# Recurrence of a delta-rule mixer: the two chains' level products issued chain by chain instead of kind by kind

## The chip, the cores and the metric

The kernel runs on one core of a Trainium2 chip. The metric is the device time of one execution in microseconds (us), lower is better. PE is the matmul engine (TensorE), DVE is VectorE, ACT is ScalarE, POOL is GpSimd, SP issues the DMAs.

## The reference

A block of two layers at 1024 tokens and width 1024. Layer 0 mixes tokens with a gated linear recurrence (eight heads of 64, run forwards and backwards) beside a dilated attention; layer 1 mixes with a Fourier transform; a convolved gated feed-forward follows each. The change touches the recurrence alone:

```python
def step(state, inp):
    r_t, w_t, k_t, v_t, kk_t, a_t = inp
    sk = jnp.einsum('bhij,bhj->bhi', state, kk_t)
    state = (state * w_t[:, :, None, :]
             - sk[..., :, None] * (kk_t * a_t)[:, :, None, :]
             + v_t[..., :, None] * k_t[:, :, None, :])
    y = jnp.einsum('bhij,bhj->bhi', state, r_t)
    return state, y
...
for d in range(2):
    ...
    y = y + wkv7_scan(rh, hs(decay), kd, vh, kk, ah, reverse=(d == 1))
```

## The kernel before

The engines run programs of their own, in order, and wait for each other by semaphores. The order of work is written out by hand in nested loops of each engine's program. In the function `recurrence` the 1024 steps are cut into 16 chunks of 64, and two chunks make a **pair step**, m = 0 to 7 (`NPAIR` is 8). Within a pair step there are two **chains**, g = 0 (forwards) and g = 1 (backwards), which share no data.

In a chunk the delta rule needs the inverse of a unit triangular 64x64 matrix, for 8 units (heads times halves) and 2 chunks. It is built up from 2x2 blocks (`X1`, `U1`) in five **levels**, i = 0 to 4 (`LEVELS` = 2, 4, 8, 16, 32). One level of one chain is, in this order of dependence:

- X product on PE (`level_x`, L1553): the chunk's matrix times the inverse so far, which is read from `T` (from `X1` at level 0). It writes PSUM bank 3 of the chain.
- XL copy on DVE (`level_x`, L1807): a predicated copy of bank 3 into `XL`.
- T product (L1572) and then U product (L1581) on PE (`level_tu`): both need the XL copy and the U copy of the level below.
- T copy on DVE (`level_t`, L1813 at level 0, L1815 at levels 1 to 3), for the next level's X product.
- U copy on ACT (`level_u`, L1668 at level 0, L1670 above).

Level 4 has no T product and no T copy. Each of these products is 32 matmul records in the trace for one chain: 64x64 weights, moving operands 32 columns wide, and 64 wide for T and U at level 0.

Beside the levels the engines prepare the next pair step's inputs (**side work**), for each chain: DVE `f_scan` (L1839), `f_centre` (L1845, L1847), `f_shift` (L1852), `f_alphas` (L1860 to L1864) and `f_nbetas` (L1869), handed out by `beside(m, slot)` in ten slots, slot 0 ahead of the pair step; ACT `f_rates` (L1690, four for each chain) and `f_exps` (L1698 to L1702); POOL `f_products` (L1745, L1746), behind `f_rates`, and `f_outputs` (L1752, L1755), behind `f_exps`. In pair step 7 there is none.

After the levels each pair step has `solve` (L1590), `carry` (L1599) and, for each chunk and chain, `step` (L1612 to L1625); ahead of them `turn`, `scores`, `lower`, `values`.

Of the kernel before, what the change touches and what calls it, by code (L numbers as in the profile page):

```python
# [539 lines left out]
NPAIR = NCH // 2  # L540
# [802 lines left out]
def recurrence(nc, z_d, vr_d, lw_d, aa_d, kk_d, tab, consts, ff, ysum, low, mix_out, bon_d, gate_d, yb_d, factors):  # L1343
# [6 lines left out]
    NL = len(LEVELS)  # L1350
    UN = 2 * KU
    HC = CH // 2
    with ExitStack() as ctx:
# [50 lines left out]
        def side(c):  # L1404
            return slice((1 - c) * CH, (2 - c) * CH)
# [16 lines left out]
        def bank(g, k):  # L1422
            return pb[:, 4 * g + k, :]
# [64 lines left out]
        def _(pe):  # L1488
# [53 lines left out]
            def level_x(g, m, i):  # L1542
                b = LEVELS[i]
                src = X1[g] if i == 0 else T[g]
                if i == 0:
                    pe.wait_ge(x1_c[g], 2 * m + 2)
                else:
                    pe.wait_ge(t_c[g], 4 * m + i)
                for u in range(UN):
                    hh, f = divmod(u, KU)  # L1550
                    for c in range(2):
                        out = bank(g, 3)[side(c), u * HC:(u + 1) * HC].rearrange("p (q b) -> p q b", b=b)
                        ins = mm(out, xn[g][side(c), hh, 2 * f + c, 0:CH], cols1(src[side(c), u, :], b, 0), start=True, stop=True)  # L1553
                ins.then_inc(x_done[g], 1)
# [74 lines left out]
            for m in range(NPAIR):  # L1629
                for phase in (turn, scores, lower, values):  # L1630
                    for g in range(2):
                        phase(g, m)
                for i in range(NL):
                    for g in range(2):
                        level_x(g, m, i)
                    for g in range(2):
                        level_tu(g, m, i)
                for phase in (solve, carry):
                    for g in range(2):
                        phase(g, m)  # L1640
                for c in range(2):
                    for g in range(2):
                        step(g, m, c)

        @block.scalar
        def _(act):
            A = nc.scalar.activation

            def tokens(g, m):
                for c in range(2):  # L1650
                    act.wait_ge(turned[g], 4 * m + c + 1)
                    A(xn[g][:, :, c::2, 2 * CH:3 * CH], bank(g, c).rearrange("p (f h e) -> p h f e", f=KU, h=2), ACT.Copy).then_inc(tok_c[g], 1)
                act.wait_ge(turned[g], 4 * m + 3)
                A(units(rz[g][:, :, 0:CH]), bank(g, 2).rearrange("p (f h e) -> p h f e", f=KU, h=2), ACT.Copy).then_inc(tok_c[g], 1)
                act.wait_ge(turned[g], 4 * m + 4)
                for c in range(2):
                    src = bank(g, 3)[other(c), :].rearrange("p (f h e) -> p h f e", f=KU, h=2)
                    A(units(wv[g][other(c), c, :, :]), src, ACT.Copy).then_inc(tok_c[g], 1)

            def values(g, m):  # L1660
                act.wait_ge(mv_done[g], m + 1)
                A(rz[g][:, :, CH:2 * CH], bank(g, 2).rearrange("p (u e) -> p u e", u=UN), ACT.Copy).then_inc(mv_c[g], 1)

            def level_u(g, m, i):
                b = LEVELS[i]
                act.wait_ge(u_done[g], NL * m + i + 1)
                if i == 0:
                    A(U[g][:, :, :], bank(g, 1).rearrange("p (u e) -> p u e", u=UN), ACT.Copy).then_inc(u_c[g], 1)  # L1668
                else:
                    A(cols(U[g][:, :, :], b, 1), narrow(g, 1, b), ACT.Copy).then_inc(u_c[g], 1)  # L1670

            def solved(g, m):
                act.wait_ge(z_done[g], m + 1)
                both_banks = pb[:, 4 * g + 2:4 * g + 4, :].rearrange("p h (f n) -> p h f n", f=KU)
                A(units(zt[g][:, :, :]), both_banks[:, :, :, 0:CH], ACT.Copy).then_inc(z_c[g], 1)
                for c in range(2):
                    A(units(wv[g][side(c), c, :, :]), both_banks[side(c), :, :, CH:2 * CH], ACT.Copy).then_inc(z_c[g], 1)

            def out(g, m, c):
                n = 2 * m + c  # L1680
                act.wait_ge(step_done[g], n + 1)
                A(ysum[:, g, :, n * CH:(n + 1) * CH], bank(g, 2 * c + 1)[:, 0:KU * CH].rearrange("p (f t) -> p f t", f=KU), ACT.Copy).then_inc(y_c[g], 1)

            def f_rates(g, m):
                act.wait_ge(ka_set, 1)
                if m:
                    act.wait_ge(f_loaded[g], 80 * m)
                    act.wait_ge(f_kappa[g], m)
                for f in range(KU):
                    ins = A(kd[g][:, f, :], aa[g][:, f, :], ACT.Identity, scale=vec[:, K_A, f:f + 1], bias=rest_ka[:, f:f + 1])  # L1690
                ins.then_inc(f_rate[g], 1)

            def f_exps(g, m):
                act.wait_ge(f_centred[g], m + 1)
                if m:
                    act.wait_ge(f_rho[g], m)
                    act.wait_ge(f_ends[g], m)
                A(emid[g][:, :, :], mids[g][:, :, :], ACT.Exp, scale=DECAY)  # L1698
                A(e1[g][:, :, :], cc[g][:, :, :], ACT.Exp, scale=DECAY).then_inc(f_exp[g], 1)
                act.wait_ge(f_before[g], m + 1)  # L1700
                A(lw[g][:, :, :], lw[g][:, :, :], ACT.Exp, scale=DECAY).then_inc(f_exp[g], 1)
                A(cc[g][:, :, :], cc[g][:, :, :], ACT.Exp, scale=-DECAY).then_inc(f_exp[g], 1)  # L1702

            for g in range(2):
                f_rates(g, 0)
            for g in range(2):
                f_exps(g, 0)
            for m in range(NPAIR):
                for phase in (tokens, values):
                    for g in range(2):  # L1710
                        phase(g, m)
                for i in range(NL):
                    for g in range(2):
                        level_u(g, m, i)
                    if m + 1 < NPAIR:
                        if i == 0:
                            for g in range(2):
                                f_rates(g, m + 1)
                        elif i <= 2:
                            f_exps(i - 1, m + 1)  # L1720
                for g in range(2):
                    solved(g, m)
                for c in range(2):
                    for g in range(2):
                        out(g, m, c)
            for g in range(2):
                act.wait_ge(y_c[g], 2 * NPAIR)
# [37 lines left out]
        def _(dve):  # L1765
# [33 lines left out]
            def level_x(g, m, i):  # L1799
                b = LEVELS[i]  # L1800
                if m == 0 and i < 2:
                    dve.wait_ge(filled_p, 2)
                if m == 0 and i == 2:
                    dve.wait_ge(filled_v, 1)
                dve.wait_ge(x_done[g], NL * m + i + 1)
                mask = level[:, i, :].rearrange("p (u q b) -> p u q b", u=1, b=b).broadcast_to([P, UN, HC // b, b])
                V.copy_predicated(cols(XL[i][g][:, :, :], b, 0), mask, narrow(g, 3, b)).then_inc(x_c[g], 1)  # L1807
# [63 lines left out]
            def beside(m, slot):  # L1871

                order = ((f_scan, 0), (f_scan, 1), (f_centre, 0), (f_centre, 1), (f_shift, 0), (f_shift, 1), (f_alphas, 0), (f_alphas, 1),
                         (f_nbetas, 0), (f_nbetas, 1))
                if m + 1 < NPAIR:
                    step, g = order[slot]
                    step(g, m + 1)
# [12 lines left out]
            for m in range(NPAIR):  # L1890
                beside(m, 0)
                for phase in (scores, lower, upper):
                    for g in range(2):
                        phase(g, m)
                for i in range(NL):
                    for g in range(2):
                        level_x(g, m, i)
                    beside(m, 2 * i + 1)
                    if i < NL - 1:
                        for g in range(2):  # L1900
                            level_t(g, m, i)
                        beside(m, 2 * i + 2)
                for g in range(2):
                    carry(g, m)
                for c in range(2):
                    for g in range(2):
                        advance(g, m, c)
# [1687 lines left out]
```

## Time and profile before

| | us |
|---|---|
| median of the 3 timed runs | 2850.46 (2849.05 to 2860.39) |
| profiled execution, first to last instruction | 2846.2 |
| recurrence, from the first X product of pair step 0 to the end of pair step 7 | about 440 |
| PE busy, whole kernel | 2625.7 (92%) |

The profiled execution has no device time of its own on record; its span of 2846.2 us lies 4.3 us under the median, which is time outside the first and last instruction and the spread of runs. A busy PE in such a table only says that matmul records follow one another: they overlap in the pipeline, so what a block of matmuls costs is read from the starts of successive blocks.

### The profile page before, as it was taken

To read this page: it belongs to the slowest core of one execution; us is meant where nothing else is said; L and a number is where in the kernel's file an instruction comes from. 1 tells how busy PE (TensorE), PEld (TensorE's weight loads), DVE (VectorE), ACT (ScalarE), POOL (GpSimd) and SP (SyncE) were. 2 spreads that over 40 slices of the span, in tenths; PEclk is the share of its full clock that TensorE was granted. 3 is DMA by queue.
4 is the path that set the end of the run, shared out by engine and by line. 5 is a ranking of instruction groups with operands and counts; after the bars stand their busy time and mean duration, and the time that the engine had idled before them with its cause. 6 is when DMAs were issued, how large, how long until landed. Compare 5 with 4: busy or idle time off the path is not lost. (4 is left out here: it accounts for less than half of the span.)

```text
span 2846.2 us, 54939 instructions
## 1 busy us (share of the span) xinstructions
PE 2625.7 (92%) x23187; PEld 2149.5 (76%) x23187; DVE 1603.8 (56%) x2296; ACT 1138.0 (40%) x1802; POOL 918.1 (32%) x625
## 2 busy tenths in 40 slices
PE   5998998896999999979999999997897999999998
PEld 5776556576989888758888888875776888888887
DVE  7775532457555544666555564455655555556445
ACT  4211342553344333344444444454434444444434
POOL 2302121104112210225877770000412777773000
PEclk9999999898999999989999999997998999999999
DMA  6676434602311220422222228543122222225654
GB/s 232 229 270 215 168 133 175 186 17 64 92 48 48 71 91 27 133 80 69 89 83 77 86 90 284 169 164 109 52 92 71 89 89 74 82 89 216 191 181 145
DMA packets 295928, 346.48 MB, mean 122 GB/s; under 512 B 28384, under 2 KB 224213, under 8 KB 295685
## 3 DMA queue, kind: packets, MB, share of 16 engines
q1 hardware_dynamic: 286044, 336.64, 36.6%
q10 hardware_dynamic: 9640, 6.33, 0.7%
q8 instruction: 185, 3.03, 0.4%
q14 instruction: 59, 0.48, 0.1%
HBM read 271.58 MB, written 71.34 MB: 120 GB/s over the span
## 5 line engine op out<-in xcount | busy, mean ns | idle before, releaser
L2847 POOL TENSOR_TENSOR cg_u_lo<-cg_u_raw,cg_u_hi 128x512 fp32r<-128x512 f32 x210 | 315.2, 1509 | 146.8 <-ACT cg_u_hi L2733 146.8
L131 PE MATMUL cg_ps<-m_hi,cg_u_hi 128*128 128x512 f32 x844 | 331.2, 392 | 26.0 <-DVE cg_u_lo L2922 21.7
L133 PE MATMUL cg_ps<-m_hi,cg_u_lo 128*128 128x512 f32 x844 | 330.0, 391 | 0.0
L132 PE MATMUL cg_ps<-m_lo,cg_u_hi 128*128 128x512 f32 x808 | 315.5, 390 | 0.0
L2733 ACT ACTIVATE cg_u_hi<-cg_u_raw 128x512 fp32r<-128x512 f32 x216 | 132.1, 629 | 380.5 <-PE cg_ps L133 229.8
L131 PEld LDWEIGHTS cg_ps<-m_hi,cg_u_hi 128*128 128x128 f32 x844 | 159.7, 189 | 61.1 <-DVE cg_u_lo L2922 22.5
L131 PE MATMUL cg_ps<-over_y_tx,cg_u_hi 128*128 128x512 f32 x480 | 186.7, 389 | 0.0
L132 PE MATMUL cg_ps<-over_y_tx,cg_u_hi 128*128 128x512 f32 x480 | 186.7, 389 | 0.0
L133 PE MATMUL cg_ps<-over_y_tx,cg_u_lo 128*128 128x512 f32 x480 | 186.7, 389 | 0.0
L133 PEld LDWEIGHTS cg_ps<-m_hi,cg_u_lo 128*128 128x128 f32 x844 | 159.5, 189 | 33.5
L2899 DVE SCALAR_TENSOR_TENSOR cg_z<-cg_ps,top_conv_f,cg_z 128x1023 f32<-128x1023 f32 x88 | 113.0, 1284 | 115.1 <-ACT cg_z L2757 115.1
L132 PEld LDWEIGHTS cg_ps<-m_lo,cg_u_hi 128*128 128x128 f32 x808 | 152.7, 189 | 31.8
L2847 POOL TENSOR_TENSOR cg_u_lo<-cg_u_s,cg_u_hi 128x512 fp32r<-128x512 f32 x80 | 103.7, 1296 | 63.5 <-ACT cg_u_hi L2733 63.5
L1745 POOL TENSOR_TENSOR rw_kd<-rw_kd,att_kx 128x512 f32<-128x512 f32 x16 | 24.7, 1543 | 280.1 <-ACT rw_kd L1690 280.1
L2902 DVE SCALAR_TENSOR_TENSOR cg_z<-cg_ps,top_conv_f,cg_z 128x1023 f32<-128x1023 f32 x88 | 112.9, 1283 | 3.1
L131 PE MATMUL za_ps<-h_hi,za_w_hi 128*128 128x512 f32 x256 | 103.7, 405 | 8.2 <-POOL za_w_lo L1029 8.2
L2757 ACT ACTIVATE cg_z<-cg_ps,top_conv_f 128x1024 f32<-128x1024 f32 x88 | 98.1, 1115 | 21.0 <-DVE cg_ps L2959 11.6
L132 PEld LDWEIGHTS cg_ps<-over_y_tx,cg_u_hi 128*128 128x128 f32 x480 | 90.1, 188 | 18.7
L133 PEld LDWEIGHTS cg_ps<-over_y_tx,cg_u_lo 128*128 128x128 f32 x480 | 90.1, 188 | 18.7
L131 PEld LDWEIGHTS cg_ps<-over_y_tx,cg_u_hi 128*128 128x128 f32 x480 | 90.1, 188 | 18.7
L131 PE MATMUL cg_ps<-over_f_d_hi,cg_a_hi 128*128 128x512 f32 x248 | 97.4, 393 | 6.3 <-DVE cg_a_lo L2918 6.3
L132 PE MATMUL za_ps<-h_lo,za_w_hi 128*128 128x512 f32 x256 | 100.9, 394 | 0.0
(475 smaller groups left out, 6515.2 us busy)
## 6 DMA issues: line engine op xcount, KB each, us to landing
cg_u_raw<-in_ffn_up SPq DMA_DIRECT2D x88, 512.0 KB, 5.1
cg_u_raw<-in_ffn_down SPq DMA_DIRECT2D x64, 512.0 KB, 4.7
qkv_mw<-in_ada_w SPq DMA_DIRECT2D x12, 2048.0 KB
over_f_d_raw<-in_ffn_down SPq DMA_DIRECT2D x48, 512.0 KB, 5.2
scr_act<-cg_z SPq DMA_DIRECT2D x44, 512.0 KB, 2.7
qkv_mw<-in_ada_w SPq DMA_DIRECT2D x8, 1024.0 KB, 11.4
next_w<-in_mix_in SPq DMA_DIRECT2D x16, 512.0 KB, 6.6
za_out<-in_ada_w SPq DMA_DIRECT2D x8, 1024.0 KB
```

Of the source, the lines that this page charges most:

```text
L131: nc.tensor.matmul(out, a_hi, b_hi, start=first, stop=False)
L132: nc.tensor.matmul(out, a_hi, b_lo, start=False, stop=False)
L133: return nc.tensor.matmul(out, a_lo, b_hi, start=False, stop=last)
L1745: TT_(kd[g][:, :, :], kd[g][:, :, :], kx[g][:, :, :], ALU.mult).then_inc(f_kd[g], 1)
L2733: A(u_hi[:, n % RING], source(g, i), ACT.Copy).then_inc(uhi_done, 1)
L2757: A(z[:, x, :], both(g, x), ACT.Copy, scale=conv_cols[:, 1, g + x * FT:g + x * FT + 1]).then_inc(mid_done, 1)
L2847: G.tensor_tensor(u_lo[:, n % RING], source(g, i), u_hi[:, n % RING].bitcast(F32), ALU.subtract).then_inc(ulo_done, 1)
L2899: V.scalar_tensor_tensor(z[:, x, 1:S], both(g, x)[:, 0:S - 1], conv_cols[:, 0, c:c + 1], z[:, x, 1:S], ALU.mult, ALU.add).then_inc(left_do ...
L2902: V.scalar_tensor_tensor(z[:, x, 0:S - 1], both(g, x)[:, 1:S], conv_cols[:, 2, c:c + 1], z[:, x, 0:S - 1], ALU.mult, ALU.add).then_inc(con ...
```

## The change

PE: the X product of level i+1 of a chain no longer waits in the order for the T and U products of both chains; it stands directly behind its own chain's. DVE: a chain's T copy, one slot of side work and its XL copy of the next level stand together, chain 0 and then chain 1. ACT: `f_rates` of a chain stands directly behind that chain's U copy of level 0, and `f_exps` of both chains stand at level 1 (chain 1's stood at level 2). No instruction is added or removed.

```diff
@@ tensor @@
+                for g in range(2):
+                    level_x(g, m, 0)
                 for i in range(NL):
                     for g in range(2):
-                        level_x(g, m, i)
-                    for g in range(2):
                         level_tu(g, m, i)
+                        if i + 1 < NL:
+                            level_x(g, m, i + 1)
@@ scalar @@
                 for i in range(NL):
                     for g in range(2):
                         level_u(g, m, i)
-                    if m + 1 < NPAIR:
-                        if i == 0:
-                            for g in range(2):
+                        if m + 1 < NPAIR:
+                            if i == 0:
                                 f_rates(g, m + 1)
-                        elif i <= 2:
-                            f_exps(i - 1, m + 1)
+                            elif i == 1:
+                                f_exps(g, m + 1)
@@ vector @@
-                for i in range(NL):
+                for g in range(2):
+                    level_x(g, m, 0)
+                beside(m, 1)
+                for i in range(NL - 1):
                     for g in range(2):
-                        level_x(g, m, i)
-                    beside(m, 2 * i + 1)
-                    if i < NL - 1:
-                        for g in range(2):
-                            level_t(g, m, i)
-                        beside(m, 2 * i + 2)
+                        level_t(g, m, i)
+                        beside(m, 2 * i + 2 + g)
+                        level_x(g, m, i + 1)
```

PE, pair step 0, levels 0 to 2. The last digit of a name is the chain, the digit behind XL is the level; U10 and U11 are the `U1` tiles of chains 0 and 1.

```order
 L1572 MATMUL rw_pb<-rw_XL0_0,rw_U10 64x64 x16
 L1581 MATMUL rw_pb<-rw_U10,rw_XL0_0 64x64 x16
+L1553 MATMUL rw_pb<-rw_T0,rw_xn0 64x32 x16
 L1572 MATMUL rw_pb<-rw_XL0_1,rw_U11 64x64 x16
 L1581 MATMUL rw_pb<-rw_U11,rw_XL0_1 64x64 x16
-L1553 MATMUL rw_pb<-rw_T0,rw_xn0 64x32 x16
 L1553 MATMUL rw_pb<-rw_T1,rw_xn1 64x32 x16
 L1572 MATMUL rw_pb<-rw_XL1_0,rw_U0 64x32 x16
 L1581 MATMUL rw_pb<-rw_U0,rw_XL1_0 64x32 x16
+L1553 MATMUL rw_pb<-rw_T0,rw_xn0 64x32 x16
 L1572 MATMUL rw_pb<-rw_XL1_1,rw_U1 64x32 x16
 L1581 MATMUL rw_pb<-rw_U1,rw_XL1_1 64x32 x16
```

Chain 0's X product moved ahead of chain 1's T and U products; between the T product of chain 0 and the X product that reads its copy there is now one block of matmuls (U), where there were three.

DVE, the same place, before:

```order
L1807 COPY_PREDICATED rw_XL0_1<-rw_level,rw_pb 128x128x2
L1839 SCALAR_TENSOR_TENSOR rw_cc1<-rw_reset_row,att_lw1 128x512
L1813 COPY rw_T0<-rw_pb 128x512
L1813 COPY rw_T1<-rw_pb 128x512
L1845 COPY rw_mids0<-rw_cc0 128x8
L1847 TENSOR_TENSOR rw_cc0<-rw_cc0,rw_mids0 128x512
L1807 COPY_PREDICATED rw_XL1_0<-rw_level,rw_pb 128x64x4
L1807 COPY_PREDICATED rw_XL1_1<-rw_level,rw_pb 128x64x4
```

and with the change (lines from L1807 on are one higher):

```order
L1808 COPY_PREDICATED rw_XL0_1<-rw_level,rw_pb 128x128x2
L1840 SCALAR_TENSOR_TENSOR rw_cc1<-rw_reset_row,att_lw1 128x512
L1814 COPY rw_T0<-rw_pb 128x512
L1846 COPY rw_mids0<-rw_cc0 128x8
L1848 TENSOR_TENSOR rw_cc0<-rw_cc0,rw_mids0 128x512
L1808 COPY_PREDICATED rw_XL1_0<-rw_level,rw_pb 128x64x4
L1814 COPY rw_T1<-rw_pb 128x512
L1846 COPY rw_mids1<-rw_cc1 128x8
L1848 TENSOR_TENSOR rw_cc1<-rw_cc1,rw_mids1 128x512
L1808 COPY_PREDICATED rw_XL1_1<-rw_level,rw_pb 128x64x4
```

Every T copy but the first now has an XL copy and a slot of side work directly ahead of it.

## Rows read from the trace of the kernel before

**Rows 1.** The page: the span.

```profile
span 2846.2 us, 54939 instructions
```

**Rows 2.** Whom PE waited for, over the recurrence: us in total, times, longest.

```profile
PE rw_pb L1572 <- DVE rw_XL L1807: 15.2, 8, 2.1
```

**Rows 3.** Timeline, pair step 2, level 0: start us, us, what, [idle before].

```profile
799.87 1.15 PE L1572 MATMUL rw_pb<-rw_XL,rw_U 64*64 64x64 f32 x32 [2.06 <-DVE rw_XL L1807]
800.10 1.18 DVE L1839 TENSOR_TENSOR_SCAN rw_cc<-rw_reset_row,att_lw 128x512 f32<-128x512 f32 x1
800.82 1.13 PE L1581 MATMUL rw_pb<-rw_U,rw_XL 64*64 64x64 f32 x32
801.21 0.65 DVE L1813 COPY rw_T<-rw_pb 128x512 f32<-128x512 f32 x1
801.99 0.60 ACT L1668 ACTIVATE rw_U<-rw_pb 128x512 f32<-128x512 f32 x1 [5.21 <-PE rw_pb L1581]
802.92 0.69 DVE L1813 COPY rw_T<-rw_pb 128x512 f32<-128x512 f32 x1 [1.06 <-PE rw_pb L1572]
803.62 2.04 PE L1553 MATMUL rw_pb<-rw_T,rw_xn 64*64 64x32 f32 x64
803.73 0.69 DVE L1847 TENSOR_TENSOR rw_cc<-rw_cc,rw_mids 128x512 f32<-128x512 f32 x1
804.35 3.17 ACT L1690 ACTIVATE rw_kd<-att_aa,rw_rest_ka,top_vec 128x128 f32<-128x128 f32 x8
806.06 1.27 POOL L1745 TENSOR_TENSOR rw_kd<-rw_kd,att_kx 128x512 f32<-128x512 f32 x1 [41.60 <-ACT rw_kd L1690]
```

**Rows 4.** Timeline of the same pair step, levels 2 and 3.

```profile
809.20 2.06 PE L1553 MATMUL rw_pb<-rw_T,rw_xn 64*64 64x32 f32 x64
812.93 1.13 PE L1572 MATMUL rw_pb<-rw_XL,rw_U 64*64 64x32 f32 x32
814.10 0.42 DVE L1815 COPY rw_T<-rw_pb 128x256 f32<-128x256 f32 x1 [1.30 <-PE rw_pb L1572]
814.80 2.06 PE L1553 MATMUL rw_pb<-rw_T,rw_xn 64*64 64x32 f32 x64
815.97 0.45 DVE L1807 COPY_PREDICATED rw_XL<-rw_level,rw_pb 128x256 f32<-128x256 uint32 x1 [0.38 <-PE rw_pb L1553]
```

**Rows 5.** Timeline of pair step 0, levels 1 and 2: DVE, POOL and PE.

```profile
696.49 1.27 POOL L1745 TENSOR_TENSOR rw_kd<-rw_kd,att_kx 128x512 f32<-128x512 f32 x1 [19.48 <-ACT rw_kd L1690]
696.52 1.25 DVE L1845 COPY rw_mids<-rw_cc 128x8 f32<-128x8 f32 x1
697.71 1.27 POOL L1746 TENSOR_TENSOR att_aa<-att_aa,att_kk 128x512 f32<-128x512 f32 x1
697.81 1.71 DVE L1847 TENSOR_TENSOR rw_cc<-rw_cc,rw_mids 128x512 f32<-128x512 f32 x1
699.44 0.74 DVE L1815 COPY rw_T<-rw_pb 128x256 f32<-128x256 f32 x2
699.91 1.94 PEld L1553 LDWEIGHTS rw_pb<-rw_T,rw_xn 64*64 64x64 f32 x64 [0.21 <-DVE rw_T L1815]
```

**Rows 6.** Timeline of pair step 2, level 3: chain 1's `f_alphas` beside POOL.

```profile
817.34 1.27 POOL L1755 TENSOR_TENSOR lt_low<-rw_kd,rw_cc 128x512 f32<-128x512 f32 x1
817.40 1.24 DVE L1862 COPY rw_ends<-rw_e 128x4 f32<-128x4 f32 x1
```

**Rows 7.** Windows over level 0 of pair steps 0, 2 and 6; the column behind POOL is the granted clock.

```profile
688.00:694.00 6.00, 5.34 (x127) 5.37 (x129) 3.42 (x6) 0.60 (x1) 0.00 (x0) 0.72 0.01 3
799.00:805.00 6.00, 5.13 (x177) 5.16 (x177) 4.56 (x9) 1.74 (x4) 0.00 (x0) 1.00 0.01 3
1023.00:1029.00 6.00, 4.90 (x120) 4.93 (x122) 3.67 (x6) 0.60 (x1) 0.00 (x0) 0.72 0.01 3
```

**Rows 8.** Timeline of pair step 3: the first T and the next X product.

```profile
855.21 1.15 PE L1572 MATMUL rw_pb<-rw_XL,rw_U 64*64 64x64 f32 x32 [2.06 <-DVE rw_XL L1807]
860.51 2.04 PE L1553 MATMUL rw_pb<-rw_T,rw_xn 64*64 64x32 f32 x64
```

## Prediction

> **What bounds the kernel now.** I read the page first for the span, 2846.2 us [rows 1], then the waits of PE over the recurrence, then timelines of single pair steps, and last the granted clock. Everything that the change moves lies in the levels, so the question is who ends last there.
>
> The waits say: PE. Over all eight pair steps it waited 15.2 us, in 8 waits, for the first XL copy of level 0, once for each pair step and ahead of the first T product [rows 2]. DVE is busy there with the copies of `upper`; the change leaves that place as it is. The only other wait of PE on level work is one of 0.21 us [rows 5]. Inside the levels PE never stops: the double X block of level 2 starts at 809.20 and that of level 3 at 814.80 [rows 4], 5.60 us for six blocks (two X, two T, two U), so 0.93 us for a block; the levels of a pair step are 26 such blocks (4 at level 0, 6 at each of levels 1 to 3, 4 at level 4), some 24 us. From the first T of level 0 to the first X of level 1 it is 803.62 - 799.87 = 3.75 us for four blocks [rows 3], the same pace. So the levels are a stream of equal PE blocks without a gap, and their order decides nothing so long as each block's operand is there in time. The reader should see this before anything else: a reordering can't shorten a stream that has no gap; it can only open gaps or not.
>
> **What the change moves, and its cost.** PE, DVE and ACT do the same instructions; only order changes. Three things follow.
>
> First, the cover of the T copy. Before, a chain's T product was followed by three blocks (chain 0) or two (chain 1) before the X product that reads it. Now it is one, U. The path: a T product's block starts at 812.93 and DVE starts its copy at 814.10 after idling, 1.17 us later, and the copy takes 0.42 [rows 4]; PE went on at 699.91, just behind the first of two T copies, which started at 699.44 and took about 0.42 [rows 5], so a release costs about 0.05 to 0.1. Sum 1.17 + 0.42 + 0.1 = 1.69 us, against two blocks (T, U), 2 x 0.93 = 1.86. It fits by 0.17 us if DVE is free at that moment. The Trainium skill, "TensorE: Matmul & The Clock Gate", section "Back-to-back issue gap", puts the floor of small matmuls at about 25 ns; by it a block of 32 would last 0.80 us, the cover would be 1.60, and every X product would wait some 0.1 us. The rows say 29 ns (0.93 / 32), so that wait isn't counted.
>
> At level 0 it doesn't fit. The scan of chain 1 (L1839) stands ahead of the first T copy as before, and that copy ends at 801.21 + 0.65 = 801.86, 1.99 us after the T block's start [rows 3]. With the release the X product can start at about 2.1 where PE is ready at 1.88: 0.2 to 0.26 us lost. The second copy of level 0 is 0.69 long [rows 3]: 1.17 + 0.69 + 0.1 = 1.96 against 1.86, 0.1 lost. Together about 0.35.
>
> Second, side work now stands between the T copy of one chain and that of the other. I lay the new order out on a line, from the start of the first T block (t = 0), in pair step 2. Between a chain's T copy and the point at which the next T copy is due DVE has a full half level (three blocks, 2.8 us), less the two copies of 0.4: about 1.9 us for the side work. Most slots are one operation of 0.69 [rows 3], but DVE operations with SBUF operands wait for POOL's. A clean one takes 0.69 [rows 3]; in pair step 0 the pair L1845, L1847 took 1.25 and 1.71, from 696.52 to 699.52, each until the end of a POOL product that started as it did [rows 5], and L1862, 128x4 elements, took 1.24 behind POOL's product of 1.27 [rows 6]. The Trainium skill, "SBUF — State Buffer", section "SBUF: two separate sides", has the rule: VectorE with two SBUF inputs, or in a two-port mode, and GpSimd take the shared ports by turns for a whole instruction. The rows agree.
>
> Third, and this decides where those collisions fall: ACT now does `f_rates` of chain 0 straight behind its U copy. That copy ends at about t = 2.7 (801.99 + 0.60), and half of the 3.17 us of L1690 is 1.6, so POOL's first product starts at t = 4.3. Before, it started at 806.06, t = 6.19 [rows 3], just behind L1845. Now:
>
> - DVE's second T copy ends at t = 4.9; chain 1's `f_centre` comes next, at 4.85, inside POOL's two products (4.3 to 5.6 to 6.8). This is pair step 0's pattern: L1845 until 5.6, L1847 until 7.3, 2.5 us in all. The XL copy goes to 7.7, the next T copy (due at 7.1) to 8.05, and the X product of level 2, due at 7.85, starts at 8.15: **0.3 us lost**.
> - `f_shift`, one operation and one POOL wait, at most 0.69 + 1.27 = 1.96, about fits its 1.9. Nothing.
> - `f_alphas` of chain 0, behind the T copy of level 2, at t = 13.4. `f_exps` run earlier now, and POOL's `f_outputs` of both chains run through, from about 10.3 to 15.7. L1860 waits for one of them, L1862 for the next (1.24), L1864 takes about 0.7: until about 16.3 instead of 14.4. XL copy to 16.6, chain 1's T copy to 16.95, X product at 17.05 where PE is ready at 16.5: **0.5 us lost**.
> - Later slots meet an idle POOL. Level 4, `solve` and what follows are as before. Nothing.
>
> Sum for a pair step at full clock: 0.35 + 0.3 + 0.5 = 1.15, say 1.2 us. Pair step 7 has no side work and counts nothing. The clock splits the other seven: PEclk over level 0 is 0.72 in pair steps 0 and 6 and 1.00 in pair step 2 [rows 7], four with 0.72 in all (0, 3, 4, 6). There, after a pause of 2.06 us ahead of the first T, part of the four blocks of 64 columns runs at 1.2 GHz: 860.51 - 855.21 = 5.30 us in pair step 3 [rows 8], against 3.75, so 1.55 lost. In such a step T and U of level 0 are slower, DVE and ACT have more time, and the stalls above come to between 0 and 1.0 us; I take 0.6. In return an X block of 32 columns (which needs 32 x 27 = 0.85 us even at 1.2 GHz, under its 0.93) now lies inside the slow stretch, which ends by time and so covers less of the wide blocks: about 0.4 us back.
>
> Total: 3 x 1.2 + 4 x (0.6 - 0.4) = 3.6 + 0.8 = **4.4 us**. Bounds: below, no stall at all and 1.6 us back; above, each centre and each alphas slot at its worst, both operations of both chains waiting out a POOL product of up to 1.7 us (L1847 took 1.71 [rows 5]), about 2 us for a pair step, 14 us.
>
> Profiled execution: 2846.2 + 4.4 = 2850.6. The median is 4.3 us above the span, so the predicted time is 2850.5 + 4.4 = **2855 us**. 0.5%, about what a measurement of this kernel tells from no change, is 14 us, 2 us for each of seven pair steps.
>
> **Rivals.**
>
> *Nothing happens* (the change doesn't do what it says). PE has no gap to close, and the collisions find room: the T copy is in time because DVE's small operation gets in just ahead of a POOL product and the large one waits for one product only. For it: only one PE wait for a T copy in the whole trace, 0.21 us, although there the pair took 3.0 us [rows 5]. Against it: that wait had three blocks of cover, now one. Time 2850.5 - 1.6 to 2850.5 + 1, so 2849 to 2851.5.
>
> *Slower past 0.5%: the late T copy.* If every slot behind a T copy (centre, shift, alphas, twice each level) meets a running POOL product and each multi-operation slot waits twice, DVE runs late against PE at three levels. A late T copy costs PE its lateness one to one, with no cover beyond 0.17 us. Three such places at 0.7 to 0.9 us for each chain give 2.1 to 2.7 us for a pair step, 15 to 19 us: 2866 to 2870. It decides from 2 us a pair step up. For it: POOL's eight products now run nearly back to back from t = 4.3 to 15.7. Against it: `f_shift` slots have 1.9 us of room, and a pair step has only two slots of more than one operation for each chain.
>
> *Faster by the clock.* PEclk at level 0 is 0.72 or 1.00 as the pause falls, in four of eight pair steps [rows 7]. Shifted starts could turn any of them: 4 x 1.55 = 6.2 us less if none is left, so with the stalls 2849, without them 2843 to 2844; as much more if all eight are slow, 2861. Under 0.5% by itself either way.
>
> **How the numbers follow.** Stalls as summed, 2852 to 2859: 0.56. Nothing, 2849 to 2852: 0.20. Clock in our favour, 2843 to 2849: 0.10. Past 0.5% slower: 0.12. Past 0.5% faster, for reasons not seen: 0.02. Same 0.86, slower 0.12, faster 0.02. The range 2846 to 2864 leaves out the slow rival and half of the clock's case; the likeliest case alone is 2852 to 2859.
>
> **What would show it.** PE waits of L1553 on DVE's T copy (L1814, L1816), none longer than 1 us, in pair steps 0 to 6 and next to none in 7, where the level 0 wait can only be 0.1. Chain 1's L1846 and L1848 together at 2.5 us or more. POOL's first product about 1.9 us earlier against the first T product. Wait for the first XL copy still 2.06 us, eight times. Wrong would be: a block pace other than 0.93 us, X products that wait over 1 us, or another stage whose length changes.

## The result, and the profile after

The changed kernel takes 2858.78 us in the median of 20 runs (2848.62 to 2872.90), the kernel before 2851.51 us in the median of 20 on the same chip (2841.77 to 2862.02). The ratio is 1.0029, 95% interval 1.0019 to 1.0040: 8.3 us slower (0.0029 x 2851.5), between 5 and 11. That is a real loss and a small one, inside the 0.5% that was called no change. A second set of 12 runs of the same changed kernel gave 1.0016 [1.0003, 1.0029]; weighted by their intervals the two make 1.0024, about 7 us.

The page gives the span, against [rows 1].

```profile
span 2854.6 us, 54939 instructions
```

8.4 us more, and the tempting reading is that these are the change. They aren't. The first T product of pair step 0 starts at 696.26 here:

```profile
696.26 1.17 PE L1572 MATMUL rw_pb<-rw_XL,rw_U 64*64 64x64 f32 x31 [2.06 <-DVE rw_XL L1808]
```

In the profile of before it starts at 688.66, so 7.6 of the 8.4 us lie ahead of the recurrence, in code that no line of the diff touches. In the first 300 us the granted clock (behind PE's busy time) is 0.92 here and 0.96 there:

```profile
0.00:300.00 300.00, 252.43 (x1054) 0.92 0.71 233
```

```profile
0.00:300.00 300.00, 254.89 (x1073) 0.96 0.72 238
```

In two more profiles of the kernel before it starts at 700.67 and 693.53, in a second of the changed one at 694.48: this stretch scatters by more than the change is worth. One pair of profiles can't say what this change costs; the levels have to be measured by themselves. I take the time from the first T product of level 0 to the first product of `solve`, summed over eight pair steps: 202.25 us before, 209.69 us after. In two more profiles of the kernel before it is 202.7 and 200.65, in a second of the changed one 210.46. Mean of three 201.9, of two 210.1: **8.2 us more in the levels**, near the 7 of the timed runs.

The waits of PE over the recurrence, total, times, longest, against [rows 2]:

```profile
PE rw_pb L1572 <- DVE rw_XL L1808: 16.0, 8, 2.1
PE rw_pb L1553 <- DVE rw_T L1816: 2.0, 7, 0.4
```

The first row is the old pause ahead of level 0, eight times as before: 2.04 to 2.06 us in six pair steps of each, and shorter in pair steps 5 and 6 (1.15 and 1.73 before, 1.70 and 1.96 here), which is the difference between 15.2 and 16.0. The second is new: X products that wait for a T copy, in pair steps 1, 2, 4 and 6 here. A row of waits counts only idle time between records that overlap by some 0.2 us, so it understates each stall. Pair step 2, below, shows them whole; it answers to [rows 3].

```profile
808.11 1.15 PE L1572 MATMUL rw_pb<-rw_XL,rw_U 64*64 64x64 f32 x32 [2.06 <-DVE rw_XL L1808]
809.06 1.13 PE L1581 MATMUL rw_pb<-rw_U,rw_XL 64*64 64x64 f32 x32
810.16 1.12 PE L1553 MATMUL rw_pb<-rw_T,rw_xn 64*64 64x32 f32 x32
811.11 1.13 PE L1572 MATMUL rw_pb<-rw_XL,rw_U 64*64 64x64 f32 x32
...
812.43 1.27 POOL L1746 TENSOR_TENSOR rw_kd<-rw_kd,att_kx 128x512 f32<-128x512 f32 x1 [43.60 <-ACT rw_kd L1692]
812.90 0.83 DVE L1846 COPY rw_mids<-rw_cc 128x8 f32<-128x8 f32 x1
...
813.76 1.71 DVE L1848 TENSOR_TENSOR rw_cc<-rw_cc,rw_mids 128x512 f32<-128x512 f32 x1
...
815.73 0.41 DVE L1816 COPY rw_T<-rw_pb 128x256 f32<-128x256 f32 x1
...
816.19 1.12 PE L1553 MATMUL rw_pb<-rw_T,rw_xn 64*64 64x32 f32 x32 [0.17 <-DVE rw_T L1816]
```

Read the starts. 808.11 to 809.06 is a block, 0.95; 809.06 to 810.16 is 1.10, a block and 0.15 us of waiting behind the scan, with no wait in the row. Then POOL's first product stands at 812.43 - 808.11 = 4.32 after the first T; the small centre operation of chain 1 takes 0.83 and the large one 1.71 behind POOL's two products; the T copy of level 1, due at 815.2, starts at 815.73; the X product starts at 816.19, 2.20 after its T block (813.99 in the trace) instead of 1.86. Later in the same pair step, against [rows 4] and [rows 6]:

```profile
821.44 1.10 DVE L1861 TENSOR_TENSOR lt_ff<-rw_ends,rw_emid 128x4 f32<-128x4 f32 x1
...
822.48 1.26 POOL L1756 TENSOR_TENSOR lt_low<-rw_kd,rw_cc 128x512 f32<-128x512 f32 x1
822.53 1.24 DVE L1863 COPY rw_ends<-rw_e 128x4 f32<-128x4 f32 x1
...
823.69 0.68 DVE L1865 TENSOR_TENSOR lt_low<-att_kk,att_lw 128x512 f32<-128x512 f32 x1
...
824.62 0.41 DVE L1816 COPY rw_T<-rw_pb 128x256 f32<-128x256 f32 x1
...
825.08 1.12 PE L1553 MATMUL rw_pb<-rw_T,rw_xn 64*64 64x32 f32 x32 [0.30 <-DVE rw_T L1816]
```

The alphas of chain 0 take from 821.44 to 824.37, 2.93 us for what chain 1's do in 0.90 with POOL idle (824.95 to 825.85 in the trace), and the X product behind starts 2.33 after its T block (822.75 in the trace), 0.47 late.

Last the granted clock at level 0 (the column behind PE's busy time), against [rows 7]; of eight pair steps seven look like the first and third row, one like the second.

```profile
696.00:702.00 6.00, 5.74 (x141) 0.72 0.03 5
808.00:814.00 6.00, 5.89 (x194) 1.00 0.01 3
864.00:870.00 6.00, 5.81 (x146) 0.72 0.01 3
```

Before it was four of eight. The pair steps with level times (us) are, before: 26.52, 24.26, 24.26, 25.91, 25.56, 25.50, 25.65, 24.59; after: 25.99, 26.70, 25.69, 26.50, 26.55, 25.90, 26.76, 25.60. (The 25.50 holds 1.2 us of pauses in which PE waited for nothing that the profile shows, the 26.52 some 0.6, and the 25.69 has 0.30 of them just ahead of `solve`.)

### The profile page after: what moved, and what is told of

It is laid out like the page before. It is cut to its first block and busy times, and to the rows that moved or that the text cites. A ratio compares the mean times of both kernels' runs of the same rounds, so it can differ in the third digit from the quotient of the medians.

```text
span 2854.6 us, 54939 instructions
## 1 busy us (share of the span) xinstructions
PE 2632.4 (92%) x23187; PEld 2155.3 (76%) x23187; DVE 1616.7 (57%) x2296; ACT 1139.0 (40%) x1802; POOL 917.1 (32%) x625
```

## Experiments

"Half-clock time" below is worked out from rows like the three above, one for each microsecond of the recurrence: twice the missing part of PEclk, summed. It is 17.0 us in the profile of before and 23.9 after. "Clean" is a pair step whose level 0 ran at PEclk 1.00 and that has no pause without a releaser. Theory A in the expectations says that late T copies are the cost, theory B that the clock is.

**How far profiles scatter (before_2, before_3, after_2).** The two kernels again, with no edit.

> The kernel before, unchanged, for a second profile. I compare level time: from the first T product of level 0 to the first solve product, summed over the eight pair steps. It was 202.3 us in the first profile of before and 209.7 in that of the changed kernel. Theory A (late copies): level time again near 202, every pair step without a wait for a T copy, 24.3 us at full clock and 25.5 to 26 with the granted clock at half over level 0. Theory B (clock): how many of the eight pair steps have the half clock over level 0 is chance for either kernel; it was 4 in before and 7 in the changed kernel, and then this run may well show 6 or 7 and a level time of 205 to 207.

Measured: 2854.73 us in one run; levels 202.7 us, clean pair steps 24.26 to 24.64, half-clock time 17.0 us, in pair steps 3 to 7 instead of 0, 3, 4 and 6.

> The kernel before against itself, for the mean granted clock of its runs. Ratio 1.000 within 0.002. Theory A: the changed kernel pauses a little more, so its clock is lower only because of that: mean clock of before 0.960 to 0.963 over its runs, against 0.959 (median of 20) for the changed kernel. Theory B: before has clearly fewer half clock stretches, 0.964 or more.

Measured: 2850.19 us, ratio 1.0005 [0.9989, 1.0021]; levels 200.65 us, half-clock time 17.1 us; level 0 ran slow in pair steps 5 to 7. The mean granted clock, for which this run was made, decides nothing: 0.9619 over 80 runs of before, 0.9606 over 32 of the changed kernel, a difference of 0.0013 with a standard error of 0.0008.

> The changed kernel again, for a second profile and more runs. Ratio 1.003 within 0.002, level time 207 to 211 us. Theory A: pair steps 0 to 6 take 1.2 to 1.4 us more in the levels than those of before at the same clock. Theory B: seven or eight of the eight pair steps at half clock over level 0 again; if it is four or five, the seven of the first profile were chance.

Measured: 2856.89 us, ratio 1.0016 [1.0003, 1.0029]; levels 210.46 us, the two clean pair steps 25.39 each, half-clock time 27.3 us. Which pair steps go slow changes from execution to execution, but the shortest clean pair step takes 24.26 us in each profile of before, and after it takes 25.39 (25.69 less the 0.30 ahead of `solve` in the first profile). So 1.13 us for a clean pair step belong to the change.

**Only PE's order (pe_only).** DVE and ACT as before, so a T copy stands behind both XL copies and the side work of its level.

```diff
@@ tensor, from the kernel before @@
+                for g in range(2):
+                    level_x(g, m, 0)
                 for i in range(NL):
                     for g in range(2):
-                        level_x(g, m, i)
-                    for g in range(2):
                         level_tu(g, m, i)
+                        if i + 1 < NL:
+                            level_x(g, m, i + 1)
```

> PE in the new order, DVE and ACT in the old one. Theory A: the cover of the T copy is one block, and now a slot of side work and both XL copies stand ahead of both T copies on DVE, so the chain 0 copy comes late at every level: 0.3 us at level 0, 0.2 to 1.8 at level 1, 0.2 at level 2, about 1.2 at level 3, in pair steps 0 to 6. 2 to 3.5 us a pair step, 14 to 24 us in all, ratio 1.005 to 1.008, waits of L1553 for the T copy of some 10 us or more. Theory B: if the change's cost is the clock at level 0 and not the copies, this costs no more than the full change, ratio 1.003.

Measured: 2901.21 us, ratio 1.0175 [1.0147, 1.0203], 50 us slower, far above the expectation. The waits explain only a fifth of it:

```profile
PE rw_pb L1553 <- DVE rw_T L1817: 11.1, 7, 1.8
```

The timeline behind the wait in pair step 2 has the rest:

```profile
824.86 1.21 PE L1553 MATMUL rw_pb<-rw_T,rw_xn 64*64 64x32 f32 x32 [0.69 <-DVE rw_T L1817]
825.87 1.90 PE L1572 MATMUL rw_pb<-rw_XL,rw_U 64*64 64x32 f32 x32
827.58 1.90 PE L1581 MATMUL rw_pb<-rw_U,rw_XL 64*64 64x32 f32 x32
829.28 1.91 PE L1553 MATMUL rw_pb<-rw_T,rw_xn 64*64 64x32 f32 x32
```

```profile
815.00:824.00 9.00, 8.71 (x290) 1.00 0.01 4
826.00:841.00 15.00, 15.00 (x286) 0.50 0.04 12
```

The clock falls to 1.2 GHz (PEclk 0.50) within 1 us behind the wait and stays there to the end of the levels, and a block then starts every 1.71 us, not every 0.93. In the other six pair steps that have side work the wait is 1.7 to 1.8 us long, comes later, and 10 to 14 us at 1.2 GHz follow. Half-clock time is 99.0 us against 17.0, so 82 us more at half speed, which is 41 us lost; with the 11.1 us of waits that makes 52, and 50 were measured. This overthrew a sentence of the prediction as well: a block of 32 columns does not keep its pace at 1.2 GHz.

**Only ACT's order (act_only).** PE and DVE as before.

```diff
@@ scalar, from the kernel before @@
-                    if m + 1 < NPAIR:
-                        if i == 0:
-                            for g in range(2):
+                        if m + 1 < NPAIR:
+                            if i == 0:
                                 f_rates(g, m + 1)
-                        elif i <= 2:
-                            f_exps(i - 1, m + 1)
+                            elif i == 1:
+                                f_exps(g, m + 1)
```

> ACT in the new order, PE and DVE in the old one: POOL's first product starts some 1.9 us earlier against level 0 and all f_exps are at level 1. Theory A: with two or three blocks of cover nothing on PE is late, level time 202 to 206, no wait for a T copy over 0.3 us, ratio 1.000 within 0.001. Theory B: the order of PE at level 0 is the old one, so the number of pair steps with the half clock is as in before, ratio 1.000 as well. A ratio of 1.003 would say that ACT's and POOL's early work is the cost by itself.

Measured: 2855.91 us, ratio 1.0018 [0.9994, 1.0041], which decides nothing. The trace is clearer. Clean pair steps take 24.50 to 24.65, 0.2 to 0.4 above the 24.26 of before, but where level 0 runs at 1.2 GHz, POOL's earlier product meets chain 0's centre (pair step 4):

```profile
923.72 1.27 POOL L1744 TENSOR_TENSOR rw_kd<-rw_kd,att_kx 128x512 f32<-128x512 f32 x1 [44.07 <-ACT rw_kd L1690]
923.83 1.19 DVE L1844 COPY rw_mids<-rw_cc 128x8 f32<-128x8 f32 x1
...
925.05 1.71 DVE L1846 TENSOR_TENSOR rw_cc<-rw_cc,rw_mids 128x512 f32<-128x512 f32 x1
...
927.25 1.12 PE L1572 MATMUL rw_pb<-rw_XL,rw_U 64*64 64x32 f32 x32 [1.20 <-DVE rw_XL L1806]
```

The XL copies stand behind the centre and the T product waits 1.20 us. Some 3 us later the clock falls and stays down to the end of the levels and beyond, so that the levels of this one pair step take 40.31 us:

```profile
931.00:959.00 28.00, 28.00 (x531) 0.50 0.20 56
```

Pair step 2 has the same wait with 0.96, and there the clock stayed up behind it. Half-clock time is 58.0 us, though this profile is of an execution well above the kernel's median (2876.55), so I take the mechanism from it and no total. I had expected no such wait: the early `f_rates` can cost PE in the old order of DVE too.

**The new order with `f_rates` as late as before (rates_late).**

```diff
@@ scalar, from the changed kernel @@
-                        if m + 1 < NPAIR:
-                            if i == 0:
-                                f_rates(g, m + 1)
-                            elif i == 1:
-                                f_exps(g, m + 1)
+                        if m + 1 < NPAIR and i == 1:
+                            f_exps(g, m + 1)
+                    if m + 1 < NPAIR and i == 0:
+                        for g in range(2):
+                            f_rates(g, m + 1)
```

> The changed kernel with f_rates of both chains back behind both U copies of level 0; f_exps stay at level 1. POOL's first product then starts some 7.4 us behind the first T product instead of 4.3, behind chain 1's f_centre, and its products no longer run through to f_alphas. Theory A (late copies): the waits at levels 2 and 4 go, 0.35 us at level 0 stays: levels 24.6 us in a pair step at full clock (25.7 in the changed kernel), no profile row of PE waiting for L1816's copy, ratio 1.000 to 1.002. Theory B (the half clock over level 0 is what costs): as the changed kernel, 1.003.

Measured: 2853.98 us, ratio 1.0004 [0.9988, 1.0020]. No wait of PE for a T copy is left. In the clean pair step 2, which starts at 805.30, chain 1's centre runs free and POOL starts at t = 7.3:

```profile
810.09 0.16 DVE L1846 COPY rw_mids<-rw_cc 128x8 f32<-128x8 f32 x1
810.28 0.69 DVE L1848 TENSOR_TENSOR rw_cc<-rw_cc,rw_mids 128x512 f32<-128x512 f32 x1
812.62 1.27 POOL L1746 TENSOR_TENSOR rw_kd<-rw_kd,att_kx 128x512 f32<-128x512 f32 x1 [42.27 <-ACT rw_kd L1692]
```

That pair step's levels take 24.55. So of the change's 1.13 us, 0.3 (24.55 - 24.26) is the tight cover at level 0 and 0.84 (25.39 - 24.55) is DVE held by POOL. The alphas of chain 0 still meet POOL, but wait once instead of twice: their first operation starts at 818.27, 0.22 us ahead of POOL's product at 818.49, and the T copy behind them is in time. That is a narrow escape, as split_new_rates below shows. In total its levels are 207.5 us, with 34.2 us of half-clock time; its interval overlaps that of after_2, measured beside it, so its gain over the changed kernel is seen in the clean pair step, in the waits that are gone and in the ratio to before, not in a comparison of medians.

**POOL's products made short (pool_narrow).** The changed order, with three of POOL's four products for a chain cut down to a few tokens in the inputs of pair steps 2 to 7; the kernel leaves out the rest of these products, and `f_nbetas`' own (`aa`) stays whole.

```diff
@@ gpsimd, from the changed kernel @@
-                TT_(kd[g][:, :, :], kd[g][:, :, :], kx[g][:, :, :], ALU.mult).then_inc(f_kd[g], 1)
+                w = slice(0, P if m < 2 else 8)
+                TT_(kd[g][:, :, w], kd[g][:, :, w], kx[g][:, :, w], ALU.mult).then_inc(f_kd[g], 1)
                 TT_(aa[g][:, :, :], aa[g][:, :, :], kk[g][:, :, :], ALU.mult).then_inc(f_nb[g], 1)
...
+                w, v = slice(0, P if m < 2 else 8), slice(0, CH if m < 2 else 4)
...
-                TT_(rho_of(g, m), rx[g][:, :, :], e1[g][:, :, :], ALU.mult).then_inc(f_rho[g], 1)
+                TT_(rho_of(g, m)[:, :, w], rx[g][:, :, w], e1[g][:, :, w], ALU.mult).then_inc(f_rho[g], 1)
...
-                TT_(kappa_of(g, m), halves(kd[g][:, :, :]), halves(cc[g][:, :, :]), ALU.mult).then_inc(f_kappa[g], 1)
+                TT_(kappa_of(g, m)[:, :, :, v], halves(kd[g][:, :, :])[:, :, :, v], halves(cc[g][:, :, :])[:, :, :, v], ALU.mult).then_inc(f_kappa[g], 1)
```

> The changed kernel with six of the eight POOL products of each pair step 8 tokens (rho, kappa: 8 and 2 x 4) instead of 128 wide from the side work of pair step 2 on: the rest of those factors is left as it was, so the computation of pair steps 2 to 7 is not the reference's. DVE's side work then waits for POOL far less. Theory A: the waits at levels 1 to 3 go, those of level 0 (0.35 us) stay: pair steps 1 to 6 at full clock take 24.6 to 24.8 us in the levels where the changed kernel took 25.7, level time 4 to 5 us less than the changed kernel's, ratio to before 1.001. Theory B: the clock alone: level time as in the changed kernel within 1 us, 1.003.

Measured: 2851.17 us, ratio 1.0000 [0.9982, 1.0019]. The clean pair step 4 takes 24.54, as in rates_late: only the 0.3 at level 0 is left. One DVE operation still waits there for the product that stayed whole (chain 1's small centre operation, 1.05 us), and no PE wait follows from it. Two edits that shorten DVE's waits for POOL in different ways give the same number. The sum of the levels missed its expectation all the same: 215.1 us, 5 more than in the changed kernel and not 4 to 5 less, with 47.8 us of half-clock time, in a profiled execution (2866.18) well above the kernel's median; so here too only the clean pair step is evidence. A surprise lies in pair step 0, whose POOL work is whole. Behind a late X product of chain 1 at level 3 the clock fell:

```profile
708.67 1.12 PE L1553 MATMUL rw_pb<-rw_T,rw_xn 64*64 64x32 f32 x32 [0.43 <-DVE rw_T L1818]
...
711.62 1.91 PE L1553 MATMUL rw_pb<-rw_T,rw_xn 64*64 64x32 f32 x32
713.33 1.90 PE L1572 MATMUL rw_pb<-rw_XL,rw_U 64*64 64x32 f32 x32
715.04 1.90 PE L1581 MATMUL rw_pb<-rw_U,rw_XL 64*64 64x32 f32 x32
```

```profile
711.00:717.00 6.00, 6.00 (x126) 6.00 (x123) 2.25 (x5) 0.40 (x2) 0.00 (x0) 0.53 0.61 173
```

1.71 us for a block again (713.33 to 715.04), after a shown wait of only 0.43. That pair step's levels took 31.59. A wait alone doesn't decide it: pair step 1 of `after` had one of 0.44 at the same place, pair step 2 one of 0.30, and nothing followed. Pair step 4 of act_only is the other such case.

**The pause ahead of level 0 cut (upper_split, upper_split_2).** The kernel before, with DVE's `upper` copies of chain 1 behind the first XL copy of chain 0. Nothing else is moved.

```diff
@@ vector, from the kernel before @@
-                for phase in (scores, lower, upper):
+                for phase in (scores, lower):
                     for g in range(2):
                         phase(g, m)
                 for i in range(NL):
                     for g in range(2):
+                        if i == 0:
+                            upper(g, m)
                         level_x(g, m, i)
```

> The kernel before with one other move: on DVE each chain's XL copy of level 0 directly behind its own upper copies, instead of both XL copies behind both chains' upper copies. The first T product no longer waits for chain 1's two upper copies (2 x 0.73 us), so the pause of 2.06 us ahead of it shrinks to 0.3 to 0.6 us, eight times: 12 to 14 us less. Theory B adds that the half clock over level 0 follows that pause: with a short pause it goes, in five of eight pair steps, 1.6 us each, and the sum is 20 us, ratio 0.993. Without a tie between pause and clock (theory A alone) the ratio is 0.995 to 0.996 and half of the pair steps still show 0.72.

> The kernel of upper_split again (the kernel before with each chain's first XL copy behind its own upper copies), as the reference for the next two. Both theories: ratio 0.993 to 0.995, pauses ahead of the first T product of 0.54 us, and at most one or two of eight pair steps with the half clock over level 0.

Measured: 2833.47 us, ratio 0.9939 [0.9921, 0.9957], and 2834.37 us, 0.9945 [0.9924, 0.9966]: 16 to 17 us faster than the kernel before. The wait ahead of the first T product:

```profile
PE rw_pb L1572 <- DVE rw_XL L1807: 4.3, 8, 0.5
```

```profile
683.00:689.00 6.00, 5.45 (x185) 1.00 0.01 3
```

The pause goes from 2.06 to 0.54 us in most pair steps; in the sum of the row it falls from 15.6 us (15.2, 15.7 and 15.8 in the three profiles of before) to 4.3, 11.3 us less. The half clock over level 0 is gone, in all 16 pair steps of the two profiles, where 12 of 24 had it before: pause and clock are tied, as theory B said. (Half-clock time in the recurrence is 3.4 us, behind the levels of pair step 6, and 0.0 in the second profile.) The levels go from 201.9 to 198.8 and 198.6, 3 us less and not more, since a clean pair step takes 24.53 instead of 24.26: chain 1's T product of level 0 now starts 2.13 us behind chain 0's instead of 1.89. Sum 14.4 us of the measured 16 to 17; the rest isn't placed. These are the fastest times of the study.

**The changed order without the pause (split_new, split_new_rates).** `upper` of chain 1 goes behind chain 0's first XL copy, and chain 0's T copy ahead of chain 1's; in the second kernel `f_rates` is late as in rates_late too.

```diff
@@ vector, from the changed kernel @@
-                for phase in (scores, lower, upper):
+                for phase in (scores, lower):
                     for g in range(2):
                         phase(g, m)
-                for g in range(2):
-                    level_x(g, m, 0)
+                upper(0, m)
+                level_x(0, m, 0)
+                upper(1, m)
+                level_t(0, m, 0)
+                level_x(1, m, 0)
                 beside(m, 1)
                 for i in range(NL - 1):
                     for g in range(2):
-                        level_t(g, m, i)
+                        if i + g:
+                            level_t(g, m, i)
```

> The changed kernel with the same move on DVE, and chain 0's first T copy ahead of chain 1's first XL copy, so that the short pause of 0.54 us is kept. Here the half clock is out of play, so the difference to upper_split is the cost of the late copies alone. Theory A: late copies cost 0.8 us at levels 0 and 1 (T copy 0.25, scan and centre ahead of the next 0.5) and 0.3 and 0.5 behind POOL's products: levels 25.4 to 25.8 us against 24.5, 8 us in all, ratio 0.996 to 0.998 to before. Theory B (the clock is most of the change's cost): with no half clock the changed order costs 2 us or less, ratio 0.994 to 0.995.

Measured: 2836.56 us, ratio 0.9948 [0.9930, 0.9965]. Levels 203.54 us against 198.8 and 198.6 of upper_split: 4.8 us more, and a usual pair step takes 25.36 against 24.53. The new order costs 0.8 us for a pair step here as well, with no half clock over level 0 mixed in (the 10.3 us of half-clock time lie elsewhere):

```profile
PE rw_pb L1553 <- DVE rw_T L1814: 2.0, 6, 0.3
PE rw_pb L1553 <- DVE rw_T L1816: 1.2, 6, 0.2
```

The first row has nothing to do with POOL: chain 1's T copy of level 0 stands behind chain 1's scan and chain 0's centre and starts at 801.54, 1.65 us behind its T block (799.89 in the trace) instead of 1.17. The second is the alphas behind POOL. So here the 0.8 is made up otherwise than in the changed kernel. The timed runs lie 2 to 3 us apart, inside the intervals; the ratio is where theory B had it, the 4.8 us lie between the 8 of theory A and the 2 of theory B, and the times neither confirm nor refute them.

> split_new with f_rates of both chains behind both U copies of level 0, as in rates_late. Theory A: the two waits behind POOL's products (0.8 us a pair step) go, those of level 0 stay: levels 24.8 to 25.2 us, 5 us less than split_new, ratio 0.995 to 0.996. Theory B: as split_new within 1 us.

Measured: 2838.68 us, ratio 0.9960 [0.9949, 0.9972]; usual pair steps 25.5 to 25.7, half-clock time 0.0. The expectation missed: the stall at the alphas stayed, and the levels are no shorter (203.9 us).

```profile
808.18 1.27 POOL L1753 TENSOR_TENSOR lt_low<-att_rx,rw_e 128x512 f32<-128x512 f32 x1
808.47 1.00 DVE L1861 TENSOR_TENSOR lt_ff<-rw_ends,rw_emid 128x4 f32<-128x4 f32 x1
...
809.46 1.24 DVE L1863 COPY rw_ends<-rw_e 128x4 f32<-128x4 f32 x1
...
812.01 1.12 PE L1553 MATMUL rw_pb<-rw_T,rw_xn 64*64 64x32 f32 x32 [0.20 <-DVE rw_T L1816]
```

Late rates push POOL's outputs later too, and here `f_alphas` meets them twice: its first operation comes 0.29 us behind POOL's product (808.47 and 808.18), where in rates_late it came 0.22 ahead. A fix that only shifts POOL works or fails by a few tenths of a microsecond.

## Why the prediction was right, and where its sizes were off

The verdict (within 0.5%), the side of it (a small loss) and the range 2846 to 2864 hold, and 2858.8 stands 3.8 above the predicted 2855. The loss itself, 4.4 us in the prediction, was 7 to 8: the sum left the half clock out, as a lottery, and one of its terms was mis-sized. Step by step:

- *PE's levels are a stream without a gap, so a reordering can only open gaps.* Right. The block pace is still 0.93 to 0.95, the pause ahead of level 0 is unchanged (2.06 in six pair steps of eight; the "eight times" of the prediction was not so in before either, 1.15 and 1.73 in pair steps 5 and 6), and no order made a pair step's levels shorter than 24.2 us.
- *Level 0 misses by 0.35.* Right: 0.3, from the clean pair steps of rates_late and pool_narrow, which have nothing else.
- *POOL's first product moves to t = 4.3, chain 1's centre takes 2.5 us behind it, 0.3 lost; the alphas of chain 0 lose 0.5.* Right: 4.32; 0.83 and 1.71 for the centre; 2.20 and 2.33 us for a T and a U block where 1.86 is room enough, so 0.34 and 0.47 lost. With shorter waits for POOL both are gone (rates_late, pool_narrow). The sum for a clean pair step, 1.15 to 1.2, measured 1.13.
- *In pair steps that go slow at level 0, stalls of 0.6 less 0.4 back, net 0.2.* This term was mis-sized. The means of such pair steps are 25.9 before (26.52, 25.91, 25.56, 25.65) and 26.4 after (the six of 0.72 and 0.75 ahead of pair step 7), 0.5 more, so the stalls were about as assumed (between none, in pair steps 0 and 5, and some 0.8) and the 0.4 back was wrong. It rested on an X block of 32 columns that keeps its 0.93 at 1.2 GHz: such a block takes 1.71 (pe_only, pool_narrow), as long as one of 64 columns there. There is no cheap block to put under the slow stretch, so nothing comes back. With 3 x 1.2 + 4 x 0.5 the sum is 5.6 us, not 4.4.
- *The clock, priced at 1.55 us for a pair step and called a lottery with either sign.* The size is right (25.9 - 24.3 = 1.6), the sign came out bad. Of the eight pair steps four, five and three began slow in the three profiles of before, seven and six in those of after: 2.5 more, 4.0 us. With the stalls of the seven that have side work, now 1.5 clean and 5.5 slow on average, 1.5 x 1.2 + 5.5 x 0.5 = 4.6, that makes 8.6, against the 8.2 us in the levels. Whether the new order makes the slow start likelier or whether five profiles just fell so is **not settled**: half-clock time was 17.0, 17.0 and 17.1 before, 23.9 and 27.3 after, 34.2 in rates_late, which looks like a cause; but in pe_only, with the new order on PE, only two of eight pair steps began slow, and I ran nothing that shifts level 0 in time and leaves the rest.

Of the rivals, "nothing happens" fell with the waits; "slower past 0.5%" named the right mechanism, and its price of 2 us for a pair step was not reached, since a shift slot (one operation, 1.18 and 1.52 us long here) has its room. Where the copies do come later than that, in pe_only, the loss is 50 us: the rival's one-to-one price for lateness was far too low, because it left the clock out.

## What to carry to other kernels

Where one engine's stream has no gap, a new order can't gain there; look instead for the pause that the stream starts with: cutting it was worth 16 us here, while the order was worth a loss of 7 to 8. Count the cover of each copy in blocks and, on the copying engine, everything that stands ahead of it in its worst form (a DVE operation behind a POOL one on SBUF), since moving one producer moves that worst form into another slot. And price a PE stall at more than its length: behind it the clock can fall, and then every block costs nearly double (1.71 against 0.93 us) until it rises.

## What the runs showed of the hardware

- With the granted clock at 0.50 (1.2 GHz), a block of 32 products of 32 columns with 64x64 weights takes 1.71 us, 53 ns each, against 0.93 us, 29 ns, at 1.00. Blocks of 64 moving columns with the same weights take no longer: 1.71 (level 0 of pair step 2 in act_only) and 0.95. So the moving columns don't set the pace of such a block at either clock; that the weights do, which PE loads anew for each product, is likely and wasn't varied.
- How long PE pauses and whether the clock then falls go together, but not by one number. Ahead of level 0, with pauses of 2.06 us in most pair steps, level 0 ran partly at 1.2 GHz in 12 of 24 pair steps before and 13 of 16 after; with pauses of 0.55 us and less, in none of 32 (the two profiles of upper_split, split_new, split_new_rates). Inside the levels: 1.7 us, in all six pair steps of pe_only that have it; shown waits of 1.20 (act_only) and 0.69 us (pe_only), the one time that each came; 0.43 us once (pool_narrow), but not 0.44 (`after`, pair step 1) nor 0.96 (act_only); 0.17 to 0.37 us, never. Pauses of 0.79, 1.22 and 1.27 us without a releaser (rates_late, split_new, pool_narrow) were followed by a fall too.
- A fallen clock at level 0 comes back within six blocks, while behind the wait in pair step 2 of pe_only PE worked 15 us without a gap at 0.50 (826 to 841), and in pair step 4 of act_only 28 us (931 to 959).
- PE has pauses of 0.2 to 2 us inside the recurrence for which the profile names no releaser, 7.2 us of them in the profile of before and 3.2 in that of after, at changing places. That hid the whole loss of the levels in the first pair of profiles: first T product of pair step 0 to that of pair step 7, 394.72 us before and 394.68 after. In the further profiles it is 388.19 and 388.23 before and 396.68 after.
